# A second PSUM bank for odd heads, an earlier turn for a gate, and another order of the first loads

## The reference

```python
# layer 0: gated linear attention beside causal attention with a forget gate (fox)
o_gla = rmsnorm(gla_chunked(q_g, k_g, v_g, gk)) * silu(g_out)      # 4 heads, chunks of 64
o_fox = softmax(q_f k_f^T / 8 + F_q - F_k, causal) v_f              # 8 heads
x = x + concat(o_gla, o_fox) @ even_w_out
# inside gla_chunked: state = exp(g_last) * state + k_to_end^T v ; o_inter = q_dec @ state

# layer 1: causal attention over selected keys with a distance bias (odd)
s = q_lat c^T / 8 + bias(dist), kept where selected and causal     # 16 heads
o = softmax(s) c ; x = x + (o @ w_uv) @ odd_w_out
```

## Time and profile before

| | |
|---|---|
| median of 3 runs | 1387.79 us (1387.4 to 1388.41) |
| profiled execution | 1387.96 us |
| its span | 1385.9 us |
| TensorE busy, share of the span | 1350.8 us, 97% |
| VectorE | 974.1 us, 70% |
| ScalarE | 677.7 us, 49% |
| GpSimd | 70.3 us, 5% |
| read from HBM over the span | 238.88 MB, 173 GB/s |

### The profile page before, as it was taken

One profiled execution on the slowest core, in us unless ns is written; L12 is line 12 of the kernel. 1 busy time (PEld: TensorE's weight loads), 2 busy tenths in 40 slices (PEclk: granted clock), 3 DMA queues, 4 the chain that ended last, 5 costly groups with the idle time before them and its releaser, 6 DMA issues.

```text
span 1385.9 us, 19410 instructions
## 1 busy us (share of the span) xinstructions
PE 1350.8 (97%) x7680; PEld 1164.1 (84%) x7680; DVE 974.1 (70%) x1328; ACT 677.7 (49%) x1057; POOL 70.3 (5%) x109
## 2 busy tenths in 40 slices
PE   8999999999999999999999999999999988999998
PEld 6988988888888888897788888888888776888886
DVE  5886777666688767658577676777666697577665
ACT  6576454443565444455554444444444456444442
POOL 0300010000000000003000000000000033000000
PEclk9999999999999999999999999999999999999999
DMA  8433546556546555454346655465654453466551
GB/s 311 154 123 122 175 174 229 183 184 195 168 154 218 193 189 188 158 182 126 120 151 212 194 192 191 162 203 198 197 183 149 150 176 86 140 205 210 190 183 46
DMA packets 67738, 241.31 MB, mean 174 GB/s; under 512 B 8015, under 2 KB 8408, under 8 KB 67648
## 3 DMA queue, kind: packets, MB, share of 16 engines
q1 hardware_dynamic: 65344, 234.19, 50.9%
q0 software_dynamic: 2016, 5.77, 1.7%
q10 hardware_dynamic: 288, 0.11, 0.0%
HBM read 238.88 MB, written 1.09 MB: 173 GB/s over the span
## 4 chain that ended last, share of the span: by engine, by line
PE 88%; DVE 6%; ACT 2%; issue 2%; DMA 1%; POOL 1%; DVEq 0%; ACTq 0%; POOLq 0%
PE pp L461 86%; PE pp L470 2%; DVE wlo L1682 2%; DVE fa L1682 1%; DVE hx L1690 1%; ACT whi L1237 1%; ACT pbuf L1388 1%; DVE pbuf L1686 1%; DMA gns<-gains 0%; ACT hx L1238 0%; ACT xn L1276 0%; DVE fa L1679 0%; DVE X L1690 0%; DVE xn L1891 0%; DMA fa<-t_rows 0%
## 5 line engine op out<-in xcount | busy, mean ns | idle before, releaser
L1682 DVE TENSOR_TENSOR wlo<-raw,whi 128x1024 fp32r<-128x1024 f32 (+1 forms) x445 | 522.9, 1217 | 149.9 <-ACT whi L1237 149.6
L461 PE MATMUL pp<-hx,whi 128*128 128x512 f32 (+1 forms) x2400 | 543.9, 362 | 7.5 <-DVE fa L1682 3.6
L461 PEld LDWEIGHTS pp<-hx,whi 128*128 128x128 f32 x2400 | 425.8, 191 | 76.8 <-issue 7.1
L1237 ACT ACTIVATE whi<-raw 128x1024 fp32r<-128x1024 f32 (+1 forms) x445 | 441.9, 1041 | 97.2 <-PE pp L461 88.6
L461 PE MATMUL pp<-whi,ra 128*128 128x512 f32 x1144 | 366.1, 391 | 0.0
L461 PE MATMUL pp<-hx,wlo 128*128 128x256 f32 x2032 | 323.3, 283 | 0.0
L461 PEld LDWEIGHTS pp<-hx,wlo 128*128 128x128 f32 x2032 | 287.0, 192 | 9.0
L461 PEld LDWEIGHTS pp<-whi,ra 128*128 128x128 f32 x1144 | 214.8, 188 | 43.9 <-issue 0.9
L461 PE MATMUL pp<-wlo,ra 128*128 128x512 f32 x572 | 222.8, 390 | 0.0
L1782 DVE TENSOR_REDUCE fa<-pp 128x512 f32<-128x1024 f32 x104 | 127.0, 1221 | 76.5 <-PE pp L461 76.5
L1237 ACT ACTIVATE ra<-fa 128x512 fp32r<-128x512 f32 x63 | 39.9, 633 | 228.3 <-DVE fa L1690 228.3
(11 more groups left out here) (175 smaller groups left out, 780.0 us busy)
## 6 DMA issues: line engine op xcount, KB each, us to landing
raw<-w_chunks SPq DMA_DIRECT2D x437, 512.0 KB, 5.2
fa<-t_rows POOLq DMA_DIRECT2D x16, 128.0 KB, 3.6
raw<-w_chunks SPq DMA_DIRECT2D x5, 256.0 KB, 6.1
fx<-x_t SPq DMA_DIRECT2D x2, 512.0 KB, 4.7
X<-x_in SPq DMA_DIRECT2D x2, 512.0 KB, 8.3
fa<-g_fin POOLq DMA_DIRECT2D x2, 512.0 KB, 5.0
fa<-f_rows POOLq DMA_DIRECT2D x8, 128.0 KB, 3.2
cst<-consts POOLq DMA_DIRECT2D x1, 576.0 KB, 7.4
```

The source lines that it names most:

```text
L461: return pe.matmul(o, lhs, rhs, start=first, stop=last, skip_group_check=True)
L1237: return act.activation(o, i, ACT.Copy, scale=1.0)
L1682: return dve.tensor_tensor(o, a, b, op)
```

## The change

**The start.** The first chunk has three halves: 512, 512 and 1024 columns. ScalarE issues the gains first and the constants second, the latter on a semaphore of their own (`s_ident`), for which GpSimd and TensorE (before `spread`) wait; ScalarE and VectorE start when the gains are there. SP issues five weight halves before the second part of the transposed input, and `X` one half earlier.

**Turned weights.** `turn_bank` gives the bank: odd heads below 4 in `fox` and below 12 in `odd` use bank 3, all others bank 6. A turn waits for the copy of the last head that used the same bank; the first one in bank 3 waits for the bank's earlier reader. `oo1.0`, which uses bank 3 later, waits for the copy of head 11.

**The states.** In pair 4 of `fox` VectorE does its side work before the conversions of weights. The steps for the last state move behind the product that empties the gate's bank.

```diff
-        step = HW // 2 if i == 0 else HW
-        halves += [(i, c, min(step, n - c)) for c in range(0, n, step)]
+        cuts = [0, HW // 2, HW, n] if i == 0 else [*range(0, n, HW), n]
+        halves += [(i, c, e - c) for c, e in zip(cuts, cuts[1:])]
...
-        TB = {"first": (3, 4), "fox": (6,), "odd": (6,)}
...
+        def turn_bank(name, h):
+            if name == "first":
+                return 3 + h % 2
+            return 3 if h % 2 and h < (4 if name == "fox" else 12) else 6
...
                 def turn_weights(h):
-                    b = tbk[h % len(tbk)]
+                    b = turn_bank(name, h)
                     src = weights_slot(name, h)
                     pe.wait_ge(s_shr, h0 + h + 1)
-                    if h >= len(tbk):
-                        pe.wait_ge(s_ptc, h0 + h + 1 - len(tbk))
+                    held = [g for g in range(h) if turn_bank(name, g) == b]
+                    if held:
+                        pe.wait_ge(s_ptc, h0 + held[-1] + 1)
+                    elif name == "odd" and b == 3:
+                        pe.wait_ge(s_kT, 4)
+                    elif name == "fox" and b == 3:
+                        pe.wait_ge(s_Fout, 1)
...
+                        if c:
+                            pe.wait_ge(s_ptc, HEAD0["odd"] + 12)
...
-                            copy(ptb[:, par, 0:tot], ps[tbk[h % len(tbk)]][:, 0:tot]).then_inc(s_ptc)
+                            copy(ptb[:, par, 0:tot], ps[turn_bank(name, h)][:, 0:tot]).then_inc(s_ptc)
...
-                act.dma_start(cst[:, 0:n], CST[:, 0:n]).then_inc(s_first, 16)
                 act.dma_start(gns[:, :], GNS).then_inc(s_first, 16)
+                act.dma_start(cst[:, 0:n], CST[:, 0:n]).then_inc(s_ident, 16)
                 act.wait_ge(s_warm, 1)
                 copy(pb[:, 512:1024], pb[:, 0:512])
-                act.wait_ge(s_first, 32)
+                act.wait_ge(s_first, 16)
                 gain = G("g_mix")
...
-                    if k < 4:
+                    if k < 3:
                         split_half()
...
+                    states = (name, p) == ("fox", 4)
+                    if states:
+                        evict((name, p, 0))
                     if causal:
                         lows(p - 1, 0)
                     lows(p - 1, 1)
-                    evict((name, p, 0))
+                    if not states:
+                        evict((name, p, 0))
...
+                def state(c):
+                    dve.wait_ge(s_kv, c + 1)
+                    if c == 0:
+                        copy(sts[:, 0].rearrange("p r c -> p (r c)"), ps[0][:, :]).then_inc(s_sts)
+                        return
+                    dve.wait_ge(s_sts, 2 * c - 1)
+                    for p in range(2):
+                        stt_(sts[:, c, p, :], sts[:, c - 1, p, :], eG[:, p, 64 * c + 63:64 * c + 64],
+                             ps[KB[c]][:, 256 * p:256 * p + 256], ALU.mult, ALU.add).then_inc(s_sts)
...
                             tt(two(gx), two(ps[2][:, :]), rbc, ALU.mult).then_inc(s_go)
+                            if g == 0:
+                                state(2)
                             dve.wait_ge(s_got, g + 1)
                             stt_(gx, gtmp, 1.0, gx, ALU.add, ALU.mult).then_inc(s_gog)
...
                         if what == "states":
-                            dve.wait_ge(s_kv, 1)
-                            copy(sts[:, 0].rearrange("p r c -> p (r c)"), ps[0][:, :]).then_inc(s_sts)
-                            for c in range(1, 3):
-                                dve.wait_ge(s_kv, c + 1)
-                                dve.wait_ge(s_sts, 2 * c - 1)
-                                for p in range(2):
-                                    stt_(sts[:, c, p, :], sts[:, c - 1, p, :], eG[:, p, 64 * c + 63:64 * c + 64],
-                                         ps[KB[c]][:, 256 * p:256 * p + 256], ALU.mult, ALU.add).then_inc(s_sts)
+                            state(0)
+                            state(1)
...
-                pool.wait_ge(s_first, 32)
-                pool.wait_ge(s_lo, 6)
+                pool.wait_ge(s_ident, 16)
+                pool.wait_ge(s_lo, 5)
...
             for j in range(5):
                 load(j)
-            load(5)
             sp.dma_start(fx[:, 1024:2048], XT[1]).then_inc(s_xt[1], 16)
             for c in range(2):
-                load(6 + c)
+                load(5 + c)
                 sp.dma_start(X[:, :, 512 * c:512 * c + 512], xv[:, :, 512 * c:512 * c + 512]).then_inc(s_x, 16)
-            for j in range(8, len(halves)):
+            for j in range(7, len(halves)):
                 load(j)
```

More of the change, by code:

```diff
@@ L220, in program @@
         s_raw = [sem(f"s_raw{i}") for i in range(NRAW)]
-        s_x = sem("s_x")
+        s_x, s_ident = sem("s_x"), sem("s_ident")
         s_xt = [sem(f"s_xt{i}") for i in range(2)]
@@ L670, in attention @@
                 causal = name != "first"
-                sbk, tbk, obk = SB[name], TB[name], OB[name]
+                sbk, obk = SB[name], OB[name]
                 def fill(p, at):
@@ L787, in first_mixer @@
                     pe.wait_ge(s_hl, n + 1)
-                    pe.wait_ge(s_lo, n + 1)
+                    pe.wait_ge(s_lo, min(n + 1, 3))
                     a = 512 * n
@@ L801, in first_mixer @@
                 pe.wait_ge(s_in, 32)
+                pe.wait_ge(s_ident, 16)
                 spread(0, 2)
@@ L1935, in first_mixer @@
                 dve.memset(pb[:, 0:512], 0.0).then_inc(s_warm)
-                dve.wait_ge(s_first, 32)
+                dve.wait_ge(s_first, 16)
                 gain = G("g_mix")
```

## The result

The changed kernel takes 1380.71 us in the median of its five runs (1376.31 to 1381.9), against 1387.79 for five runs of the kernel before: a ratio of 0.9941, with a 95% interval of 0.9922 to 0.9961. The forecast was 1377.4, the range 1373.5 to 1382. The five runs are two groups, two near 1376.5 and three near 1381, and the profiled one, 1381.71 with a span of 1379.7, is of the slower group. Four more runs of the same kernel, timed beside the second set of experiments, gave 1376.34 to 1378.06 (median 1376.69, ratio 0.9927, 0.9914 to 0.9941); the median of all nine is 1376.9.

A forecast was written before the change was run, and what follows sets the result against it. The prediction took TensorE to bound the kernel, with losses where it stands still or runs at its lower clock. Terms 0.3 + 0 + 5.4 + 4.9 = 10.6 us, from 1387.96 to 1377.4 us; range 1373.5 to 1382.

The forecast's parts named there:

- rival A: In `fox`, the clock falls at the 2.5 us stall before the inner products, costing 2.6 us: 1380.0; chance 0.20.
- The states behind the gate: Pair 4 of `fox`: TensorE's gate wait falls from 3.59 to 0.9 us, 2.8 gained, plus 2.6 from the clock: 5.4 us.
- The second bank in `odd`: Loop of `odd`: turns stop waiting for copies, VectorE's queue sets the pace, 23.32 us stretch shortens: 4.9 us gained.
- The second bank in `fox`: Loop of `fox`: two turn waits go, but the stall before the inner products grows to about 2.5 us: nothing gained.
- The start: First loads: TensorE starts 0.6 us sooner, at 8.5, at half clock, worth 0.3 us; bounds 0 to 2.8.
- B: GpSimd's masks get out of the way, some 2 us, or the start gives 2.2 instead of 0.3: 1375.5; chance 0.13.
- C: In `odd`, the weighing waits in every pair and the old period stays, gain there 3.2 us: 1379.1; chance 0.08.
- D: The clock stays down in both loops through shorter but more frequent gaps: 1409, some 21 us slower; chance 0.02.

The follow-up runs named there:

- the 27 products: The kernel before, with 27 unread products of 128x256 on TensorE in place of its wait for the gate's bank: 1382.93 us, ratio 0.9965.
- two such moves: The changed kernel with `kdc` and `ke` ahead in pair 2 of `fox` and `q3`'s product ahead in pair 5 of `odd`: 1371.21 us, ratio 0.9888.

## Why the prediction was right, and where it wasn't

The forecast, a gain of 10.6 us, is above both measurements of the change, 8.2 (5.4 to 10.8) and 10.1 (8.2 to 11.9), and inside both intervals. The first median, 1380.71, is nearest to rival A's 1380.0, and that of all nine runs, 1376.9, to the forecast's 1377.4. Of its signs two came out against it: in `odd` there is a wait of 2.02 us and a clock of 0.50 behind it, and before the inner products of `fox` the 0.50 that it had named as A's. By its steps:

**The states behind the gate, 5.4: right in mechanism, a little high in price.** The wait was predicted at 0.9 and is 0.78. The two shares are shown apart: 2.8 for the wait, by the profiles, and for the clock 1.3 to 2.5 by the products in its place, where 2.6 was predicted. The price was too high, since behind the same wait the clock was down for a shorter time in five other profiles than in the one that the prediction had. Alone the edit gave 4.2 (2.8 to 5.7). The two conversions that moved behind are covered: four in a row from 662.34 and no wait of TensorE for weights.

**The second bank in `odd`, 4.9: right as far as it went, with a step missing.** VectorE's stretch was to be 18 to 19 us long with 17.92 busy; it is 18.67 with 17.94, at a granted clock of 1.00: 4.65 us shorter. The scalings of 1.0 to 1.6 us are still there, with GpSimd busy 12.83 us: as the row had it, not shorter. But the text named "nearly 2 at the entry to pair 6" and gave that wait a price only in the slower rival. It is 2.02, the clock fell behind it in both profiles, and 1.5 us are lost there, so that the stretch as a whole gains 3.4. Waits of 1.5 and less at this place left the clock up in five profiles.

**The second bank in `fox`, nothing gained: right, but without rival A's price, which comes in some runs.** The stall was predicted at about 2.5 and is 2.61. A had 0.20 as something that happens or doesn't. In truth it happens in some executions: in 3 of 4 profiles with this stall, at 1.6 and 2.6 us in the two of the change (from the inner products to the gate's second half 12.8 and 13.9 us, against 11.2 with the clock up). The chance should have been for a share of the runs, and the forecast for a median between 1377.4 and 1380. Alone the edit lost 1.5 (0.1 to 2.8).

**The start, 0.3: too small, the term that was mis-sized.** The first product with `hx` came at 8.80, not 8.5, since the first weight part took 0.3 us longer. Nor was 9.14 the time of the old order: four other profiles with the constants first had it at 8.41 to 8.72, seven with the whole new order at 8.25 to 8.80. The DMA issues, answering to the earlier trace rows:

```profile
raw<-w_chunks SPq DMA_DIRECT2D x1, 256.0 KB, 6.1
cst<-consts ACTq DMA_DIRECT2D x1, 72.0 KB, 6.3
gns<-gains ACTq DMA_DIRECT2D x1, 39.0 KB, 4.0
```

The gains landed at 4.7, as predicted, and turned out to be worth nothing alone. What the text had put at nothing, more transfers asked for before the first wait for a slot, is what pays. In the old order the weights set the length of the start at either clock; in the new order the start is shorter unless the clock is down as long as in the profile that the prediction read. It took that one for the rule. Measured alone: 1.5 us (0.3 to 2.8), within the bounds of 0 to 2.8.

So two errors of opposite sign, a start worth 1.2 us more and falls of the clock at two new stalls that cost 1.5 to 2.6 each when they come, left the sum about right. That they cancelled is luck, and the intervals are about 2 us wide either way.

**The rivals.** B's second half, a start worth 2.2, happened in part (1.5, with 2.2 inside its interval); the scalings took what they took before. C is refuted: no wait for a copy over 1.2 us, and the stretch of VectorE 18.67, not over 20. D is refuted in its size, not in its beginning: behind the wait of 1.16 in the loop of `odd` the clock fell in four of the seven profiles with the second bank, but came back within 3.5 us each time, and cost at most 0.6.

On the rule of the Trainium skill (TensorE: Matmul & The Clock Gate, Why this matters for your kernels) that an idle stretch between bursts sends the clock back: the traces agree, and the 27 products kept it up in their profile. They add that a gap of 2.6 us isn't certain to do it, and that one of 1.16, with waits of 1.08 and 0.5 in the 7 us before it, can. On the port rule (SBUF — State Buffer, Terms): VectorE's busy time hardly changed in the shorter loop, 17.94 against 17.92; no run here took GpSimd's work away, so how much of it is locked time stays open.

## What to carry to other kernels

A wait that is taken away comes back at the next thing that TensorE needs; find that one first, and put the work that it waits for early in the other engine's queue. Here two such moves gave 5.5 us on top of the change.

Price a stall at its length plus the clock that it may take with it, as a share of the runs. Ask of each profile whether the clock happened to be up or down in it, and read a second one before you call an edit worthless: the start was the same length in the one pair at the low clock, and 0.7 to 2.5 us shorter in those at the full clock.

## What the runs showed that I had not expected

The clock falls by chance behind the same stall. At one place a wait of 1.92 us left it up and one of 1.84 brought it down; at another a wait of 2.62 left it up in one profile and brought it down in another. Behind a wait of 1.16 it fell in four profiles of seven. The wait of 3.6 did so every time, in six of six profiles, but for a shorter time in five of them. What decides it, no run here shows. Each such fall that differs between profiles is worth about 1 to 2.6 us; several of them, with the start, would make the spread between the runs of one kernel here, 5 us in the kernel before. That is an estimate from the profiles; no run shows it.
